# The two 128-token tiles of a latent pass go apart from the output projection on

## The reference

```
mix = merge_branches(...) @ w_out
x   = layer_norm(ALPHA * x + g1 * mix, ln1_g, ln1_b)
u   = layer_norm(x) * (1 + sc2) + sh2
# peer_ffn(u), for each token:
q = (u @ wq) -> 8 heads x 2 halves x 128
s1, s2 = q . k1, q . k2                  # 128 keys each
v1, i1 = top_k(s1, 16); v2, i2 = top_k(s2, 16)
top_s, pos = top_k(v1[:, None] + v2[None, :], 16)
eidx = 128 * i1[..] + i2[..];  g = softmax(top_s)
h = gelu(eu[eidx] . u);  ffn = sum (g * h) * ev[eidx]
x = layer_norm(ALPHA * x + g2 * ffn, ln2_g, ln2_b)
```

## Time and profile before

| | us |
|---|---|
| median of 3 runs | 3332.6 (3328.14 to 3336.45) |
| profiled execution, its own time | 3334.65 |
| its span, first to last instruction | 3332.8 |
| busy: PE / PE loads / DVE | 2535.4 / 1289.2 / 1962.9 |
| busy: ACT / POOL | 515.1 / 973.9 |
| HBM read | 1011.32 MB, 306 GB/s over the span |
| granted PE clock, mean | 0.76 |

### The profile page before, as it was taken

How to read it: one execution, slowest core, us unless ns; L and a number is a source line. 1 busy time by engine, 2 the same in 40 slices (tenths; PEclk the granted TensorE clock), 3 DMA queues, 4 the chain that set the end, 5 groups by cost and what they waited for, 6 DMA issues and landing times.

```text
span 3332.8 us, 32715 instructions
## 1 busy us (share of the span) xinstructions
PE 2535.4 (76%) x10880; PEld 1289.2 (39%) x10880; DVE 1962.9 (59%) x6008; ACT 515.1 (15%) x1106; POOL 973.9 (29%) x967
## 2 busy tenths in 40 slices
PE   6889983789999969658889876777988366566555
PEld 5768872243455535124444411113677011111111
DVE  4778958747544466875444455554646855555555
ACT  2151111124322111002022200001502000000000
POOL 0830000276322222323932233331000233333332
PEclk7989986695899979668889866566898555665666
DMA  7606732897899979886999999994042599989997
GB/s 301 234 29 260 300 132 112 342 380 277 349 400 377 384 297 368 323 339 256 334 388 402 410 362 398 393 401 196 26 160 95 228 372 388 407 343 403 403 405 309
DMA packets 147881, 1023.45 MB, mean 307 GB/s; under 512 B 18816, under 2 KB 19328, under 8 KB 28032
## 3 DMA queue, kind: packets, MB, share of 16 engines
q0 software_dynamic: 110592, 805.36, 60.9%
q1 hardware_dynamic: 30496, 202.36, 15.9%
q10 hardware_dynamic: 6624, 13.64, 1.1%
HBM read 1011.32 MB, written 9.96 MB: 306 GB/s over the span
## 4 chain that ended last, share of the span: by engine, by line
PE 45%; DMA 20%; DVE 19%; POOL 8%; issue 5%; ACT 3%; ACTq 0%; DVEq 0%; POOLq 0%; SPq 0%
DMA ring<-in_peer_uv,eT 20%; PE PS L1043 10%; PE PS L821 6%; DVE ring L1709 6%; POOL ring L660 5%; PE PS L978 5%; PE PS L1061 4%; PE PS L756 3%; PE PS L939 2%; PE PS L842 2%; PE PS L826 2%; PE PS L885 2%; PE PS L908 2%; DVE ring L1379 1%; POOL mix L555 1%
## 5 line engine op out<-in xcount | busy, mean ns | idle before, releaser
L1709 DVE CUSTOM_DVE_ANT_0 ring<-ring,PS 128x512 f32<-128x512 f32 x1536 | 993.2, 684 | 830.1 <-PE PS L1061 454.8
L660 POOL DMA_INDIRECT ring<-in_peer_uv,eT x768 | 726.6, 946 | 2224.0 <-PE PS L1043 1339.7
L1061 PE MATMUL PS<-xr,onesb 3*128 3x512 bf16 x1536 | 610.4, 483 | 379.1 <-DVE hcol L1709 329.1
L1043 PE MATMUL PS<-ring,zcol 128*32 128x512 f32 x3072 | 601.0, 924 | 185.9 <-DVE zcol L1719 184.6
L1061 PEld LDWEIGHTS PS<-xr,onesb 3*128 3x128 bf16 x1536 | 108.8, 96 | 959.1 <-DVE hcol L1709 474.6
L1043 PEld LDWEIGHTS PS<-ring,zcol 128*32 128x32 f32 x3072 | 104.8, 144 | 491.5 <-DVE zcol L1719 257.2
L821 PE MATMUL PS<-uT,W 128*128 128x256 f32 x1024 | 249.9, 393 | 4.3 <-issue 4.3
L1312 ACT ACTIVATE ge<-hdot 128x4 f32<-128x4 f32 x192 | 39.4, 205 | 1382.7 <-DVE hdot L1714 1371.4
L1379 DVE CUSTOM_DVE_ANT_0 ring<-ring 128x1024 f32<-128x1024 f32 x160 | 211.6, 1361 | 28.6 <-DMA ring<-in_w_rows 23.8
L821 PEld LDWEIGHTS PS<-uT,W 128*128 128x128 f32 x1024 | 193.5, 194 | 62.8 <-issue 34.7
L978 PE MATMUL PS<-uT,W 128*128 128x256 f32 x768 | 183.2, 395 | 0.0
(11 more groups left out here) (190 smaller groups left out, 2418.9 us busy)
## 6 DMA issues: line engine op xcount, KB each, us to landing
ring<-in_w_rows SPq DMA_DIRECT2D x40, 1024.0 KB, 8.0
W<-in_w_in SPq DMA_DIRECT2D x30, 1024.0 KB
W<-in_w_q SPq DMA_DIRECT2D x24, 1024.0 KB
W<-in_w_gate SPq DMA_DIRECT2D x16, 1408.0 KB
W<-in_w_gate SPq DMA_DIRECT2D x16, 1280.0 KB
W<-in_w_gate SPq DMA_DIRECT2D x16, 1024.0 KB
W<-in_w_out SPq DMA_DIRECT2D x12, 1024.0 KB
xr<-xrows ACTq DMA_DIRECT2D x768, 6.0 KB
```

The costliest lines, as they stand in the source:

```text
L660: pool.indirect_dma_start(ring[:, slot, :], None, (peer_uv0, peer_uv1)[b.l], bass.IndirectOffsetOnAxis(eT[:, f % 2, t:t + 1], 0)).then_inc ...
L1043: last = T.matmul(PS[k * NR:(k + 1) * NR, (6 + h) * 512:(7 + h) * 512], zcol[:, g % 2, k, NR - 1 - at:2 * NR - 1 - at], ring[:, slot, D + ...
L1061: T.matmul(bank(x_bank(q, n) + h), onesb[32 * k:32 * k + 3, :], xr[32 * k:32 * k + 3, g % 2, h * 512:(h + 1) * 512], start=True, stop=True)\
L1709: V.tensor_tensor_reduce(out=u_half, in0=u_half, in1=bank(x_bank(q, n) + h), scale=1.0, scalar=0.0, op0=ALU.mult, op1=ALU.add, accum_out=h ...
```

## The change

In BL0 and BL1 (`apart=True`) the two tiles are separated behind the output projection; BC0 stays as it was.

- PE, ACT and DVE each get a function `apart(b, a)`. The first tile's sum, norm, transposes and modulation go ahead of the second's; PE's query units are per tile (`unit(tt, u)`, 128 columns), and so are the scores (`scores(tt, c)`, two heads).
- The first tile is selected by two heads: as soon as the scores of a pair of heads are copied out, DVE does their top 16, candidates, decoding and one-hot sums, while PE goes on with the next units. PE does the 16 units of the first tile and 10 (AHEAD) of the second.
- Then TILE_READY. The other 6 units and 2 scores of the second tile, and its top 16 (eight steps "late", 1.2 tokens each), and then its selection over all heads (eight steps "sel", 2.5 each) are woven with tokens of the first tile.
- The query weights go into the 8 ring slots, not through `W`, so they stay for both tiles; the first 8 expert requests of the pass wait until their slot's units are done. The keys come as one more tile of `W`.
- In the last pass only tokens of the second tile alternate between two pairs of broadcast banks.
- SCRIPT: the norm of FL0 goes before the front of KV0; KV0's front has one row product per unit instead of two.
- Each tile's rows in DRAM have their own semaphore (`xs0`, `xs1`).

```diff
-SCRIPT = [("ada", 0, 0, 4), ("norm", KV0), ("ada", 0, 4, 8), ("front", KV0), ("norm", FL0), ("front", FL0), ("back", BL0),
+SCRIPT = [("ada", 0, 0, 4), ("norm", KV0), ("ada", 0, 4, 8), ("norm", FL0), ("front", KV0), ("front", FL0),
+          ("back", BL0),
...
+         "late": 1.2}
+AHEAD = 10
+LATE = 8
...
-            return 2 * (n % 2) if ORDER[q] == LAT1 else 0
+            return 2 * (n % 2) if ORDER[q] == LAT1 and n >= P else 0
...
+            def query_weights(b):
+                if b is BL0:
+                    sp.wait_ge(row_done, len(ROW_TILES))
+                else:
+                    sp.wait_ge(weighed, ORDER.index(b.f) * NG)
+                for t in range(SLOTS):
+                    sp.dma_start(ring[:, t, :], w_q[b.l, t]).then_inc(query_land[t], 16)
...
+                if b.apart and n < SLOTS:
+                    pool.wait_ge(a["wo"], a.at("wo", KD + 16 + 2 * n + 2))
...
+            def apart(b, a):                                   # PE
+                l = b.l
+                turned(2, lambda k: oT[:, k, 0:P]).then_inc(a["resT"], 1)
+                turned(0, lambda k: oT[:, k, P:TOK]).then_inc(a["resT"], 1)
...
+                for u in range(16):
+                    unit(0, u)
+                    if u % 4 == 1 and u >= 5:
+                        scores(0, u // 4 - 1)
+                    if u == 6:
...
+                        turned(0, lambda k: scratch[:, 1, k * P:(k + 1) * P]).then_inc(a["xnT"], 1)
+                    if u == 10:
...
+                        turned(0, lambda k: uT[:, k, P:TOK]).then_inc(a["urow"], 1)
+                for u in range(AHEAD):
+                    unit(1, u)
...
+                yield TILE_READY
+                for q in range(LATE):
+                    u = AHEAD + q
+                    if u < 16:
+                        unit(1, u)
+                    if u == 13:
+                        scores(1, 2)
+                    if u == 16:
+                        scores(1, 3)
+                    yield "late"
...
+                summed_row(0)                                  # DVE
+                dve.wait_ge(a["rsum"], a.at("rsum", 1))
+                stats([scratch[:, 0, :]], a["stat"], 0)
+                summed_row(1)
+                middle(0)
+                dve.wait_ge(a["rsum"], a.at("rsum", TT))
+                stats([scratch[:, 1, :]], a["stat"], 1)
+                normed(0)
+                middle(1)
+                split(0)
+                normed(1)
...
+                for c in range(4):
+                    dve.wait_ge(a["sc_s"], a.at("sc_s", c + 1))
+                    for g in (4 * c, 4 * c + 2):
+                        top16([(v16[:, g + e, :], i16[:, g + e, :], segs_a[:, c % 2, (g % 4 + e) * NKEY:(g % 4 + e + 1) * NKEY],
+                                rest_a[:, e, :]) for e in range(2)])
+                    dve.sem_inc(a["top"], 1)
+                    ch.link(V.tensor_copy(i16f[:, 4 * c:4 * c + 4, :], i16[:, 4 * c:4 * c + 4, :]))
+                    candidates(0, 2 * c, 2, cand_a)
+                    top16([(ts[:, 2 * c + h, :], pos[:, 2 * c + h, :], cand_a[:, h, :], cand_rest_a[:, h, :]) for h in range(2)])
+                    decoded(2 * c, 2, dec_a)
+                    for e in range(2):
+                        picked(0, 2 * c, 2, e, hot_a, isel_a)
+                    if c == 1:
+                        split(1)
+                joined(a, isel_a)
+                weighted(a, 0)
+                yield TILE_READY
+                for q in range(LATE):
+                    if q % 2 == 0:
+                        dve.wait_ge(a["sc_s"], a.at("sc_s", 4 + q // 2 + 1))
+                    top16([(v16[:, SEG + 2 * q + e, :], i16[:, SEG + 2 * q + e, :], segs_b[:, 2 * q + e, :], rest_a[:, e, :])
+                           for e in range(2)])
+                    yield "late"
...
+                yield from selection(a, 1, isel)
```

More of the change, by code:

```diff
@@ L347, in build @@
         row_done = sem("row_tiles_done")
+        query_land = [sem(f"query_weights_landed{k}") for k in range(SLOTS)]
         mod_s = sem("mod_ready")
@@ L624, in back @@
                         yield "out"
+                if b.apart:
+                    yield TILE_READY
+                    for q in range(LATE):
+                        yield "late"
+                    for q in range(8):
+                        yield "sel"
+                    yield TILE_READY
+                    return
                 for q in range(4):
@@ L1130, in front @@
                           "gq": lambda j: gqk[:, j, :], "gk": lambda j: gqk[:, 4, :] if s == 0 else gkc[:, :]}
+                for tt in range(TT):
+                    if a.at(f"xs{tt}", 0) > 0:
+                        act.wait_ge(a[f"xs{tt}"], a.at(f"xs{tt}", 0))
                 for n, (kind, tile, blk, dst) in enumerate(r.units):
@@ L1245, in back @@
                     yield "out"
+                if b.apart:
+                    yield from apart(b, a)
+                    return
                 for q in range(4):
@@ L1353, in normed_rows @@
                 for tt in range(TT):
-                    before = a.at("xnT", tt + 1 - TT)
+                    before = a.at("xnT", tt + 1 if a is at_of["norm", FL0] else tt + 1 - TT)
                     if before > 0:
@@ L1667, in back @@
-                    yield "sel"
-                    dve.wait_ge(a["texp"], a.at("texp", tt + 1))
-                    ch.link(V.reduce_sum(hsum[:, 1, :], ts[:, :, :], AX))
-                    ch.link(V.reciprocal(hsum[:, 1, :], hsum[:, 1, :]))
-                    V.tensor_tensor(ts[:, :, :], ts[:, :, :], hsum[:, 1, :].unsqueeze(2).to_broadcast(top),
-                                    ALU.mult).then_inc(a["sel"], 1)
-                    yield "sel"
-                    yield TILE_READY
+                    yield from selection(a, tt, isel)
@@ new lines, in selection @@
+            def selection(a, tt, index):
+                candidates(tt, 0, HEADS, cand)
+                for q in range(4):
+                    top16([(ts[:, g, :], pos[:, g, :], cand[:, g, :], cand_rest[:, g, :]) for g in (2 * q, 2 * q + 1)])
+                    yield "sel"
+                decoded(0, HEADS, dec)
+                yield "sel"
+                for e in range(2):
+                    picked(tt, 0, HEADS, e, hot, index)
+                    if e == 0:
+                        yield "sel"
+                joined(a, index)
+                yield "sel"
+                weighted(a, tt)
+                yield "sel"
+                yield TILE_READY
```

316 lines of the change are left out of this document (251 added, 65 removed).

## The result

| | before | after |
|---|---|---|
| time, median of 5 runs | 3336.5 us (3328.1 to 3340.8) | 3317.0 us (3310.6 to 3321.7) |
| ratio to before | 1 | 0.9946, 95% interval 0.9927 to 0.9966 |
| profiled execution: own time, span | 3334.65, 3332.8 | 3317.04, 3315.2 |

What follows compares the result with a forecast made beforehand. No single engine bounds the end; the last pass alone is DMA-bound, with a DMA gap before its first request. First pass -20.0 and last -19.3, together -39, gave 3295, or 3293 us against the median; range 3269 to 3316.

Steps and rivals of the forecast that it cites:

- Part 1: Both latent passes, output projection to first expert request: the request comes 36 us earlier, bounds 28 to 42.
- The rival of narrow products: Products on 128 columns get no cheaper, a unit staying at 3.45 us: time 3333, chance 0.02.
- Part 2: Second tile's selection behind the first requests: stretch of 100.6 us, 39 to 40 longer, ten tokens more done; bounds 87 to 121.
- The rival in which PE and DVE take turns: Second tile's stretch: PE's units and scores delay broadcasts, each stretch 125 us if all exposed, time 3343; chance of slower 0.06.
- the one of better interleaving: Vector and token work interleave at 1.37 a token, stretches about 11.5 us shorter: time 3263, chance 0.11.
- Part 3: Worth of ten tokens done ahead: 26.3 us in the last pass; 16.8 in the context stretch plus 1.9 for the first.
- The seam of 1.9: Behind the first pass two tokens follow and not three, saving 1.9 us.
- Part 4: One broadcast bank pair for the last pass's first 128 tokens: costs 2.6 us, bounds 0 to 5.
- one pass gives nothing: First pass's earlier requests save nothing, as context steps set their own pace up to selection: time 3313, chance 0.13.
- Part 5: Kernel start, latent norm ahead of the context K/V front, removing PE's 6.62 us wait: gain 4.5 us, bounds 0 to 6.6.
- Part 6: Query weights in ring slots, both latent passes: arrive in time, costing nothing, bounds 0 to 8 us.

Runs made afterwards that it cites:

- kernels at 0 and at 0.6 above: Fifteen kernels grouped by token credit left behind the first pass: region (first pass's second closing to context's first) 794 to 804 us at 0, 810 to 815 at 0.6.
- the first pass alone: The kernel after with the last latent pass kept whole as before, so only the first pass goes apart: 3338.8 us, ratio 1.0.

## Why the prediction was wrong, by its own steps

- **Part 1** (36 us earlier) holds in its sum and its pieces: 37.3 from the stage's own start. A quarter of the columns of selection cost what the fixed part of 0.16 us said: rounds of 14.3 for 13.9. The prediction set this against the 58 cycles of a table in the Trainium skill ("VectorE: DVE Perf Modes", the section on the TRN2 errata); the lines under that table put the measured fixed part at about 150 cycles, by an estimate with its 0.96 GHz 0.16 us, and the rows agree. The products on 128 columns took 128.4 us for 1024 passes, 125 ns each, some of them at the slower clock, against 111 in the earlier trace rows. The rival of narrow products is excluded: by it a unit would have stayed at 3.45 us, and it is 16 x 0.125 = 2.0. The Trainium skill ("TensorE: Matmul & The Clock Gate", the mechanism of packing) has a list by which loads overlap only across row groups; its text just above also allows a load into the background weight buffer. The trace disagrees with the list: in the last pass 512 such products of 128 rows have 512 loads, and the loads are hidden.
- **Part 2** (stretch 100.6) was right to 3 us, by a wrong split. Without late tokens a stretch takes 80.1 and 79.7 us and holds 17 tokens from closing to closing; with them it takes 103.2 and 103.8 and holds 27, as forecast: 2.3 to 2.4 for each of the ten, and 2.6 for each of the eight with the share of 1.0, where 1.87 stood. The rest of the stretch costs less than was put for it: 80.1 where 50.1 + 17 x 1.87 = 81.9 stood. The rival in which PE and DVE take turns (125) and the one of better interleaving (89) are both out.
- **Part 3** is the step that failed: "First pass: tokens run on beside the context pass, where the number woven per step is the same." The share per step is the same, and so is the number in the whole region, 224, but not the number in single steps: a fraction of 0.6 in credit shifts which steps get two tokens, and with it the region takes 12 to 15 us more (kernels at 0 and at 0.6 above); the prediction put this at nothing. The share of 1.0, which leaves no fraction, is the check: its span falls by 35.5 us (3332.8 to 3297.3), with 3.3 gained in the region, near the forecast's 39.3. The seam of 1.9 can't be told from this. The other half of the part holds, but for its count: the context stretch holds 5 tokens and not 6, ten fewer than before, and is 18.7 shorter, 1.87 for each, the price that was put; in the last pass the tail is 24.6 shorter for ten tokens, where 26.3 less the 2.6 of Part 4 stood.
- The rival "one pass gives nothing", 3313, came within 4 us of the time by luck, for a wrong reason. The first pass did give nothing, but not because tokens ahead ran in gaps: with no credit carried, the ahead tokens pay in the context stretch (54.7 to 39.7 with 28).
- **Part 4** (+2.6) was too much by all that shows: the tail takes 634.4 us for 229 tokens, 2.77 each, for 659.0 and 239 before, 2.76 each. With the new single pair and 239 tokens left too, three kernels (the first pass alone, and both with no late token) took 660.3, 657.1 and 660.1 us; with the old two pairs the three others took 659.0, 660.1 and 657.7.
- **Part 5** (-4.5): the wait of 6.62 is gone; the latent modulation starts at 69.85, 4.2 us earlier, and the context one at 38.49 for 36.97, 1.5 later as forecast. The row products take 205.7 us for 211.6 and stand idle for 8.3 us and not 28.6, and the first residual sum comes 4.9 us earlier:
```profile
38.49 5.66 ACT L1257 ACTIVATE uT<-PS,mod 128x128 f32<-128x128 f32 x16
...
69.85 5.69 ACT L1257 ACTIVATE uT<-PS,mod 128x128 f32<-128x128 f32 x16 [4.64 <-PE PS L765]
...
429.44 1.22 DVE L1916 SCALAR_TENSOR_TENSOR scratch<-X,PS 128x1024 f32<-128x1024 f32 x1 [3.72 <-PE PS L915]
```
- **Part 6** (nothing): the first query product starts at 447.5, 449 was forecast, and PE waits for no slot.
- **The sum.** Of the 21.7 us between -39.3 and -17.6 in the span, 17.2 are the region of Part 3, 5.8 the two stretches, 2.2 the later arrival at the last pass's closing, and 3.5 are given back by the context stretch, the start and the tail. The chance of faster was right; the range ended too low on the slow side, because it held no cost for a shifted pattern of steps.

## What to carry to other kernels

Where independent work is woven into a schedule by shares, a change of any share shifts everything behind it. Compare the pattern of steps as well as the counts, and try a few shares that leave no fraction before judging the edit: here one constant, 1.2 or 1.0, decided between a ratio of 0.9946 and one of 0.9891. Measure the price of a woven item against what it saves where it would run otherwise: here 2.3 to 2.6 us against 1.9 in the next pass's selection and 2.5 alone (24.6 us for ten in the tail), so that weaving none into the new steps did as well (0.9887). Where PE waits a few microseconds ahead of a long run of products, look for products whose operands are there already: the wait can cost the pace behind it too.

## What the runs showed of the hardware

- The same program repeats a stage closely: two kernels with a common first half show 245.40 and 245.42 us of busy PE in a stretch of 256 us. The region around it took 814.5 and 812.3.
- An idle time of 3.72 us of PE, at a granted clock of 0.50 (1.2 GHz), went with eight products of 3.75 us behind it; without it, behind a broadcast or a weighing, they took 1.97 to 1.99.
- In a region that is bound by PE (busy 97%), 3.5 us more of idle time went with 10.5 us more of busy time for nearly the same products, at a clock of 0.93 for 0.97. The ratio of three is not fixed: with nothing but the credit changed in the kernel before, 2.9 us more of idle time (247.3 less 237.3 busy) went with 2.4 more of busy time, at 0.97.
